# Third block's front: the SiLU behind the next chunk's conversion, norm groups over two chunks, 24 gate slices from the matrix stages into the scan

## The reference, cut to what matters

```
proj = h @ w_in
pool_in, qkv, z, beta_raw, a_raw, gate_a, gate_b = split(proj)
y_a = multiscale_pool(pool_in, pool_w, pool_scale)      # (window mean - x) @ pool_w, 4 windows
qkv = silu(causal_depthwise_conv(qkv, conv_w))          # 4 taps, 3072 channels
q, k = l2norm(q) * 128**-0.5, l2norm(k)                 # per head of 128, 8 heads
beta = sigmoid(beta_raw); g = -exp(a_log) * softplus(a_raw + dt_bias)
o = chunk_gated_delta_rule(q, k, v, beta, g)            # 8 chunks of 64 tokens, a scan over a state
o = rmsnorm(o) * o_norm_w * silu(z)
mixed = sigmoid(gate_a) * y_a + sigmoid(gate_b) * o
h = layer_norm(alpha * h + mixed @ w_out); ...          # then an MLP and a gate
```

## Time and profile before

| what | value |
|---|---|
| median of 3 runs | 3551.41 us |
| profiled execution | 3550.06 us, span 3548.2 us, mean granted clock 0.942 |
| PE busy | 3279.4 us, 92% of the span |
| PEld busy | 2596.0 us, 73% |
| DVE busy | 1743.6 us, 49% |
| ACT busy | 1207.2 us, 34% |
| POOL busy | 176.3 us, 5% |
| DMA | 285.20 MB, 80 GB/s |

### The profile page before, as it was taken

How to read it: one execution, slowest core, us unless ns; L and a number is a source line. 1 busy time by engine, 2 the same in 40 slices (tenths; PEclk the granted TensorE clock), 3 DMA queues, 4 the chain that set the end, 5 groups by cost and what they waited for, 6 DMA issues and landing times. The chain is left out here.

```text
span 3548.2 us, 42736 instructions
## 1 busy us (share of the span) xinstructions
PE 3279.4 (92%) x17800; PEld 2596.0 (73%) x17800; DVE 1743.6 (49%) x2592; ACT 1207.2 (34%) x1718; POOL 176.3 (5%) x174
## 2 busy tenths in 40 slices
PE   8999998889689998999899999998888889999998
PEld 6888776668468886877557788876667778778885
DVE  4447536553354445776875433335653234553434
ACT  3333342221543333333344322223553223242323
POOL 0000000210000000000000000001102331000000
PEclk9999997869899999999999999999998999899999
DMA  3225321000122254322002223221122101122222
GB/s 138 95 96 213 119 75 48 2 1 8 52 85 96 100 197 145 110 89 71 12 1 101 77 97 100 97 100 54 66 72 71 31 25 43 65 82 97 95 97 93
DMA packets 76368, 285.20 MB, mean 80 GB/s; under 512 B 8464, under 2 KB 8592, under 8 KB 75152
## 3 DMA queue, kind: packets, MB, share of 16 engines
q1 hardware_dynamic: 76176, 282.47, 23.5%
HBM read 276.15 MB, written 6.29 MB: 80 GB/s over the span
## 5 line engine op out<-in xcount | busy, mean ns | idle before, releaser
L149 DVE TENSOR_TENSOR wlo<-raw,whi 128x1024 fp32r<-128x1024 f32 x450 | 555.0, 1233 | 1252.5 <-ACT whi L144 1252.2
L144 ACT ACTIVATE whi<-raw 128x1024 fp32r<-128x1024 f32 x450 | 476.0, 1058 | 1193.4 <-PE ps L173 1189.7
L171 PE MATMUL ps<-h_hi,wlo 128*128 128x512 f32 x1800 | 725.6, 403 | 56.5 <-DVE wlo L149 20.0
L172 PE MATMUL ps<-h_lo,whi 128*128 128x512 f32 x1800 | 708.1, 393 | 0.0
L173 PE MATMUL ps<-h_hi,whi 128*128 128x512 f32 x1800 | 707.8, 393 | 0.0
L171 PEld LDWEIGHTS ps<-h_hi,wlo 128*128 128x128 f32 x1800 | 343.0, 191 | 147.6 <-issue 55.6
L172 PEld LDWEIGHTS ps<-h_lo,whi 128*128 128x128 f32 x1800 | 342.8, 190 | 74.9 <-issue 6.0
L173 PEld LDWEIGHTS ps<-h_hi,whi 128*128 128x128 f32 x1800 | 342.2, 190 | 72.8
L171 PE MATMUL ps<-mid_hi,wlo 128*128 128x512 f32 x784 | 307.4, 392 | 0.0
L173 PE MATMUL ps<-mid_hi,whi 128*128 128x512 f32 x784 | 305.0, 389 | 0.0
L172 PE MATMUL ps<-mid_lo,whi 128*128 128x512 f32 x784 | 305.0, 389 | 0.0
(11 more groups left out here) (576 smaller groups left out, 4736.3 us busy)
## 6 DMA issues: line engine op xcount, KB each, us to landing
raw<-in_wstream SPq DMA_DIRECT2D x453, 512.0 KB, 3.4
mod_ring<-in_wmod SPq DMA_DIRECT2D x48, 512.0 KB, 4.5
c_rows<-in_c_rows SPq DMA_DIRECT2D x3, 1024.0 KB, 5.6
x<-in_x_t SPq DMA_DIRECT2D x4, 512.0 KB, 7.2
x_saved<-x SPq DMA_DIRECT2D x1, 2048.0 KB, 8.9
x<-x_saved SPq DMA_DIRECT2D x1, 2048.0 KB, 9.1
mix_saved_d<-x SPq DMA_DIRECT2D x1, 2048.0 KB, 8.5
out<-x SPq DMA_DIRECT2D x8, 256.0 KB, 2.6
```

The source lines that it names most:

```text
L144: act.activation(k.whi[:, n % SPLIT, :], k.raw[:, n % RAW, :], ACT.Copy).then_inc(k.hi_ready, 1)
L149: dve.tensor_tensor(k.wlo[:, n % SPLIT, :], k.raw[:, n % RAW, :], k.whi[:, n % SPLIT, :].bitcast(F32), ALU.subtract).then_inc(k.split_read ...
L171: pe.matmul(out, wlo, hi, start=first, stop=False)
L172: pe.matmul(out, whi, lo, start=False, stop=False)
```

## The change

In the front the pool moves from before chunk 8 to before chunk 9 (`POOL_AT`), in the code and in the order of the stream. ScalarE's SiLU of chunk f - 1 is issued after the evacuation of chunk f, with a wait for the taps of chunk f - 4 ahead of the evacuation. The pairs of sums move one chunk later, Ln comes at chunks 7, 11, 15, 19 and Exp one chunk after it; the norm products follow one chunk later than before. The first eight turns wait for the norms alone. The turning of beta and g, the sums and what follows them move one gate chunk forward, the exponentials stand in the sixth gate chunk, and k's scaling is shared between the last two. The matrix stages get (2, 2, 2) slices, the scan (4, 3, 1).

```diff
+POOL_AT = 9
-    q_chunk = lambda f: b0 + 1 + f + (f >= DT)
-    pool_chunk, g0 = b0 + 1 + DT, b0 + 26
+    q_chunk = lambda f: b0 + 1 + f + (f >= POOL_AT)
+    pool_chunk, g0 = b0 + 1 + POOL_AT, b0 + 26
...
-                pe.wait_ge(normed, 2 * DT)
-                pe.wait_ge(silu_done, 3 * DT)
+                if n < DT:
+                    pe.wait_ge(normed, 2 * DT)
+                else:
+                    pe.wait_ge(silu_done, 3 * DT)
...
-                group = (f - 5) // 4
-                if f >= 5 and f % 4 in (1, 2) and group < 4:
-                    first = 4 * group + 2 * (f % 4 - 1)
+                group = (f - 6) // 4
+                if f >= 6 and f % 4 in (2, 3) and group < 4:
+                    first = 4 * group + 2 * (f % 4 - 2)
...
-                if i == 3:
+                if i == 2:
                     pe.wait_ge(g_ready, 1)
...
-                if i == 5:
+                if i == 4:
                     pe.wait_ge(g_ready, 2)
...
+            def silu(f):
+                act.wait_ge(tap_done, 4 * f + 4)
+                act.activation(qkv[:, f, :], qkv[:, f, :], ACT.Silu).then_inc(silu_done, 1)
...
+                if f >= 4:
+                    act.wait_ge(tap_done, 4 * f - 12)
                 act.activation(pre[:, f % 4, 3:], k.ps[:, f % 4, :], ACT.Copy).then_inc(pre_ready, 1)
...
-                act.wait_ge(tap_done, 4 * f + 4)
-                act.activation(qkv[:, f, :], qkv[:, f, :], ACT.Silu).then_inc(silu_done, 1)
-                if f >= 6 and f % 4 == 2 and f < 22:
-                    first = f - 6
-                    for n in range(first, first + 4):
+                if f:
+                    silu(f - 1)
+                if f >= 7 and f % 4 == 3 and f < 23:
+                    for n in range(f - 7, f - 3):
...
-                    for n in range(first, first + 4):
+                if f >= 8 and f % 4 == 0 and f < 24:
+                    for n in range(f - 8, f - 4):
                         act.wait_ge(log_ready, n + 1)
...
+            silu(3 * DT - 1)
...
-            act.wait_ge(summed, 1)
-            for t, bank, first in (...): act.activation(... ACT.Exp)
+                if i == 5:
+                    act.wait_ge(summed, 1)
+                    for t, bank, first in (...): act.activation(... ACT.Exp)
...
-                if f >= 8 and f % 4 in (0, 1):
-                    first = f - 8 + f % 4
+                if f >= 9 and f % 4 in (1, 2):
+                    first = 4 * ((f - 9) // 4) + 2 * (f % 4 - 1)
...
-                if i == 4:
+                if i == 3:
                     dve.wait_ge(rows_turned, 1)
...
-            dve.wait_ge(kept, 4)
-            dve.wait_ge(copied, 8)
-            for T in range(TT):
+                if i >= 6:
+                    dve.wait_ge(kept, 4)
+                    dve.wait_ge(copied, DT)
+                    for T in range(2 * i - 12, 2 * i - 10):
...
-            delta_matrices(k, c, q, key, v[:, 2:8, :], nbeta, g, ..., attn, bg, (4, 4, 4))
+            delta_matrices(k, c, q, key, v[:, 2:8, :], nbeta, g, ..., attn, bg, (2, 2, 2))
...
-        delta_scan_and_close(..., (3, 2, 0))
+        delta_scan_and_close(..., (4, 3, 1))
...
-        s += _dense(cut(512, 1024)) + [pooled] + _dense(cut(1536, 2048)) + _dense(cut(4624, 1024))
+        s += _dense(cut(512, P * POOL_AT)) + [pooled] + _dense(cut(512 + P * POOL_AT, 3072 - P * POOL_AT)) + _dense(cut(4624, 1024))
```

More of the change, by code:

```diff
@@ L2898, in _ @@
             for f in range(3 * DT):
-                if f == DT:
+                if f == POOL_AT:
                     pe.wait_ge(k.split_ready, pool_chunk + 1)
@@ L3001, in _ @@
                        .then_inc(copied, 1)
-            act.wait_ge(summed, 1)
[L3003 to L3006, removed]
+                if i == 5:
+                    act.wait_ge(summed, 1)
+                    for t, bank, first in ((egc[:, :, :], 7, 0), (ekg[:, :, :], 7, 32), (egl[:, 0:8:2, :], 7, 64),
+                                           (egl[:, 1:8:2, :], 6, 64)):
+                        act.activation(t, k.ps[:, bank, first:first + 32].rearrange("p (a n) -> p a n", n=8), ACT.Exp)\
+                           .then_inc(kept, 1)
         @m.block.vector
@@ L3082, in _ @@
                     dve.tensor_scalar(nbeta[:, :, :], beta[:, :, :], -1.0, None, ALU.mult).then_inc(plus, 1)
-            dve.wait_ge(kept, 4)
-            dve.wait_ge(copied, 8)
-            for T in range(TT):
-                kt = k_tok[:, T, :].rearrange("p (h n) -> p h n", n=P)
-                dve.tensor_tensor(kt, kt, bcast_last(ekg[:, T, :], P), ALU.mult).then_inc(scaled, 1)
+                if i >= 6:
+                    dve.wait_ge(kept, 4)
+                    dve.wait_ge(copied, DT)
+                    for T in range(2 * i - 12, 2 * i - 10):
+                        kt = k_tok[:, T, :].rearrange("p (h n) -> p h n", n=P)
+                        dve.tensor_tensor(kt, kt, bcast_last(ekg[:, T, :], P), ALU.mult).then_inc(scaled, 1)
 def delta_matrices(k, c, q, key, tmp, nbeta, g, at, attn, bg, slices):
@@ L3704, in deltanet @@
         for c in range(4):
-            delta_matrices(k, c, q, key, v[:, 2:8, :], nbeta, g, a_t[2 * (c % 2):2 * (c % 2) + 2], attn, bg, (4, 4, 4))
+            delta_matrices(k, c, q, key, v[:, 2:8, :], nbeta, g, a_t[2 * (c % 2):2 * (c % 2) + 2], attn, bg, (2, 2, 2))
             if c % 2:
@@ L3710, in deltanet @@
         delta_scan_and_close(k, q, key, k_tok, v_tok, xt, attn, beta, egc, egl, v, gate, h, mix_d, p_d, out, bg,
-                             (3, 2, 0))
+                             (4, 3, 1))
         assert bg.at == 8 * bg.n
```

## The result

The changed kernel takes 3518.91 us (median of 4 runs, 3515.71 to 3520.30) against 3551.94 (4 runs, 3541.09 to 3552.76): ratio 0.9913, interval 0.9896 to 0.9929, so 33.0 us less. The forecast was 3531; its own range began at 3521, the whole range at 3514.

The account below looks back on a forecast made before the run. TensorE's matmuls bound the front, with waits from a circle between ScalarE and VectorE; -10.7 - 18.0 + 3.3 - 3.7 - 13.7 + 18.9 + 4.5 = -19.4 from 3550.1 gave forecast 3531, range 3514 to 3545.

Parts of the forecast that it names:

- The bound: Third block's front: matmuls bound it where unbroken; the 40 us between TensorE's busy 222.5 and 262.5 us can be won.
- Pool: Front up to the pool: SiLU one chunk late ends the pool at 2516.8 with chunk 8 done, -10.7 us.
- rival 4: Table switches in the front cost twice their 1.28 us load, pool 3.8 us later, time 3535; chance 0.05.
- Chunks 9 to 23: Front after the pool: ScalarE and VectorE stop waiting in a circle, TensorE sets the pace, -18.0 us.
- the sign of being right: Front: chunks 9 to 23 with their sums take 92 us, one of several signs listed for a right forecast.
- Turning and rows: Front's gate chunks: turning of beta and g, moved earlier, waits 4.2 us for a chain of small operations; +3.3 us.
- End of the front: Last gate chunks: a 1.41 us wait and two of four products behind the last gate product go, -3.7 us.
- Matrix stages: Four matrix stages with 6 slices each instead of 12: pairs fall from 94.3 to 80.6 us, -13.7 us.
- Rival 1: Matrix stages run on at 1.2 GHz, so moved slices are pure load in the scan, time 3544; chance 0.12.
- Scan: Scan with 8 slices a step: +16.3 us for slices at 0.68 each, +5.0 for late residual products, less 2.4; +18.9.
- Rival 2: More than forecast: matrix stages at 72 us and the scan's residual products hidden, time 3517; chance 0.20.
- Tail: Scan's end: chunk 15's evacuation comes after the last product instead of beneath it, +4.5 us.

Follow-up runs that it names:

- front_only: The changed kernel with the old slice places, (4,4,4) in the matrix stages and (3,2,0) in the scan: 3521.18 us, front 231.5.
- silu_back: The changed kernel with the SiLU of each chunk again right behind its own taps, ahead of the next conversion: 3548.38 us, front 258.9.
- ln_exp_together: The changed kernel with the four Exp of a norm group directly behind their Ln, in one chunk: 3520.84 us, front 231.5.
- shift2: The changed kernel with two slices moved from the scan's end to the first matrix stage, (3,3,2): 3502.08 us, ratio to before 0.9858.
- slices_only: The kernel before with only the slices changed, to (2,2,2) and (4,3,1): 3552.20 us, ratio 1.0007.
- extra_slices: The kernel before with some 21 scan slices issued a second time, three a step: 3552.09 us, ratio 1.0007, scan 135.6.
- gaps_440: The changed kernel with (4,4,0) for (4,3,1) slices in a scan step's three gaps: 3521.22 us, scan 144.4.
- best: The changed kernel with (3,3,2) in the first matrix stage and g's chain in the first gate chunk, behind the copies: 3502.74 us, ratio to before 0.9869.

## Why the prediction was right, and where not

**The bound.** Right: TensorE's waits set the front. front_only has the 31 us, and silu_back takes 27.3 of them away by the one order that the argument named.

**Pool.** Forecast -10.7; the pool's products end at 2517.9 with chunk 8 done, 2522.1 before: -4.2 and one chunk of 5.4, -9.7 (the front starts 0.1 later). The first four Ln end at 2504.9, forecast 2504.1. ScalarE's sequence was conversion, evacuation, load, SiLU, load, four Exp as forecast; here it is from the conversion to the evacuation of the pool:

```profile
2504.79 1.07 ACT L144 ACTIVATE whi<-raw 128x1024 fp32r<-128x1024 f32 x1
...
2506.37 1.28 ACT L2956 ACT_TABLE_LOAD   x1
2507.66 0.63 ACT L2956 ACTIVATE qkv<-qkv 128x512 f32<-128x512 f32 x1
2508.31 1.28 ACT L2991 ACT_TABLE_LOAD   x1
2509.61 2.19 ACT L2991 ACTIVATE norm_factor<-norm_factor 128x512 f32<-128x512 f32 x4
2511.70 3.10 ACT L2967 ACTIVATE x<-ps,vecs 128x512 f32<-128x512 f32 x5
```

From 2504.79 to 2511.70 it is 6.9 us, forecast 7.0. Each function starts 1.29 or 1.30 us after its load began, and the load at 2508.31 begins 0.02 behind the SiLU's end. That refutes rival 4; the Trainium skill ("ScalarE: Activation LUTs", What ACT_TABLE_LOAD costs) adds a drain to each load, and these rows leave no room for one.

**Chunks 9 to 23.** Forecast -18.0, measured -18.2 with the pool taken out (2643.34 to 2615.53 is -27.8 in all). From the pool's end to the first turn are 97.8 us with the first gate chunk's 5.5, so the fifteen chunks and their sums took 92.3, where 92 was the sign of being right. ln_exp_together confirms that the fourth table load is hidden; a group that isn't divided is hidden as well. What the forecast did not see is that the pool's term and this one are not independent: silu_back loses both.

**Turning and rows.** Forecast +3.3, measured +0.7 (55.3 to 56.1 us). The new wait came as computed, 4.3 against 4.2. What was missed is on the other side: before, the sums in 32 tiny matmuls were followed by a chunk of 8.20 us, the larger part at half clock, after it took 5.8. The forecast had put 2 us of half clock to the 8.0 us gap and 1 us against it, and had not seen this chunk.

**End of the front.** Forecast -3.7, measured -3.8 (8.4 to 4.7).

**Matrix stages.** Forecast -13.7. The two pairs fell by 11.3 and 5.6, 16.9 in all (within the lower bound of -22; both are counted to the first product of the inversion, 1.3 us behind the ends in the earlier trace rows). Rival 1 had the stages gain nothing, so it is refuted, although their clock did stay low: 0.84 and 0.83, the second 0.91 before. Not in the sum were the inversions: the last gap of the first now ends a chunk (3.30 us idle, the stretch 3.7 longer), the second is 1.7 shorter, +2.0 together. Net -15.0. The working looked at chunk ends in the four stages and the scan only, not in the inversions between.

**Scan: the step that was mis-sized.** Forecast +18.9, measured +11.0. A step at full clock grew about as forecast, by 2.9 us: before 14.32, after 17.2 (before and after in turn below, each with a slow step ahead or behind; the third fence is a step of shift2, which has no wait).

```profile
2926.06:2945.71 19.65, 18.10 (x98) 15.55 (x97) 7.56 (x7) 6.61 (x8) 1.90 (x1) 0.80 0.08 28
2991.67:3005.99 14.32, 14.32 (x99) 12.05 (x98) 5.65 (x5) 2.41 (x4) 1.90 (x1) 1.00 0.19 59
```

```profile
2882.86:2900.15 17.29, 16.62 (x107) 13.66 (x106) 7.57 (x7) 6.48 (x9) 1.88 (x2) 1.00 0.09 30
2952.08:2971.21 19.13, 19.13 (x107) 15.80 (x106) 7.57 (x7) 6.66 (x9) 2.33 (x2) 0.86 0.08 28
```

```profile
2893.54:2910.14 16.60, 16.60 (x107) 13.66 (x107) 7.35 (x7) 6.62 (x9) 1.90 (x2) 1.00 0.11 32
```

Three slices more thus cost 2.28 us at full clock (16.60 less 14.32), 0.76 each and not 0.68. TensorE's busy time in the whole scan rose by 11.4 us, 126.3 to 137.7. The 23.3 slices added up to the last output would have been 17.7 at 0.76, an estimate, so 6.3 us come back as clock. Idle time went from 2.7 to 2.4, where the forecast had +5.0 for the residual products less the 2.4 for vn: 3.0 less. So 18.9 + 1.4 - 6.3 - 3.0 = 11.0.

The sum priced each slice at full clock and left the scan's own clock as it stood in the earlier trace rows, 0.89; the trace of the kernel before had the rows to see it in, the same state products at 1.96 us a set in one step and 3.67 in another. Rival 2 had "denser matmuls in the scan" as its reason, but put the gain to the residual products and to matrix stages of 72 us. The wait for the products was indeed less (2.4 in place of 5.0), but the stages took 80, and the larger share in the scan is clock: rival 2's time came out near for a reason that is only in part its own. slices_only (+10.3) and extra_slices (6.5 for 14.3) show it apart from the front.

Of the clock, the Trainium skill ("TensorE: Matmul & The Clock Gate", Part 1) has it that activity releases the throttled state. extra_slices agrees in its sign, 0.88 to 0.93. gaps_440 and best, with a TensorE that is never idle in the scan at 0.88 and 0.89, show that busy time alone doesn't hold it.

**Tail.** Forecast +4.5, measured +3.7 (9.1 to 12.7); w_out now waits 9.4 us for the last low part. gaps_440 takes it away, as the term's reason asks.

**Sum.** -9.7 - 18.2 + 0.7 - 3.8 - 15.0 + 11.0 + 3.7 = -31.3, with 0.3 elsewhere. Against -19.4 the difference is -11.9: scan -7.9, turning -2.6, matrix -1.3, the rest -0.1. The sign and the place of the gain were shown by runs; of the amount, 6.3 us rest on a clock that the working had held constant.

What stays open: why one execution's scan has 0.96 and another's, with the same instructions, 0.89. No experiment here controlled it. Also, the part of shift2's gain that is clock (3.3 us: state products and head sums, 29.6 to 26.3) could be smaller in another set of executions; its 7.5 us in the matrix part, 2.4 in the scan and 3.9 in the tail have named waits.

## What to carry to other kernels

A per-item loop in which one in-order engine both serves the matmuls (splits) and finishes their results (SiLU) can lock two engines in a circle; putting the finish one item late was worth 27 us here, and moving pure load between stages nothing. When matmul slices are used as filler, ask what stands behind the evacuation where their chunk ends: at the border of a stage or step it cost 3.3 us at an inversion, up to 0.7 a step and 3.7 in the tail, and two slices moved took all three away; but between two matrix stages the border was no worse than a gap just ahead of an Exp. And where a stretch shows a granted clock under full, price what is added there with a rebate as one bound, since the matmuls around it may get faster.

## What the runs showed of the hardware

TensorE's clock fell in stretches in which it never idled. In gaps_440's scan, 144.44 us busy of 144.44, the granted clock was 0.88; a step's 16 state products took 1.96 us at full clock and 3.67 in slow steps. In `best`, a gate chunk after the row sums took 8.39 us; the windows ahead of and over that chunk:

```profile
2636.00:2640.50 4.50, 4.50 (x41) 4.48 (x39) 1.82 (x2) 2.52 (x4) 0.00 (x0) 0.88 0.15 46
2640.50:2648.90 8.40, 8.40 (x27) 6.62 (x28) 0.00 (x0) 0.00 (x0) 0.00 (x0) 0.66 0.10 40
```

What TensorE did before these falls was the same kind of work: 32 sums with 8 columns here, runs of state products and outputs with 64 and 128 columns in the scan, at 1.2 GHz of 2.4 afterwards. It doesn't come with every run of them: the kernel after has the same 32 sums, and its chunk behind them took 5.8 us.
